# A mixture-of-experts layer whose 64 expert jobs are divided into 19 of 128 rows and 45 of 64 rows

## The chip, the cores and the metric

The kernel runs on one core of a Trainium2 chip. The metric is the device time of one launch in microseconds, from the first to the last work of the core. The matrix engine (TensorE) is PE in the profile, its weight loads are PEld, VectorE is DVE, ScalarE is ACT, GpSimd is POOL, and SyncE, which here only issues DMAs, is SP.

## What is computed

One layer of a decoder for 256 prompt tokens and 8 sample tokens, 264 in all, with a width of 1024. A token mixer of four branches comes first; behind it stands the mixture of experts that the change is about. All in fp32:

```python
scores = sigmoid(h @ router_w)
# 8 of 64 experts for each token, out of the 4 best of 8 groups of experts
gates  = 2.5 * scores of the chosen / their sum
hg  = einsum('nd,edf->nef', h, e_gate)      # e_gate, e_up: 64 x 1024 x 256
hu  = einsum('nd,edf->nef', h, e_up)
act = silu(hg) * hu * gates[:, :, None]
routed = einsum('nef,efd->nd', act, e_down) # e_down: 64 x 256 x 1024
x = x + gate2 * (routed + shared expert)    # then a final RMSNorm
```

With the inputs given, the routing sends between 0 and 118 tokens to an expert, 2112 in all. Nine of the 64 experts have over 64 tokens (118, 107, 106, 93, 84, 79, 76, 69, 68).

## The kernel before

The first 400 us are the token mixer, the routing and the shared expert; the change doesn't touch them. From then on the experts run as 64 jobs, one expert each, in 16 groups of `UNROLL` = 4. Groups 0, 1 and 2 are written out, 3 to 14 are a hardware loop, group 15 is written out again. Group 0 holds experts 0 to 3. All others are sorted by their token count on the chip, and `rank_of_job` tells which rank in this order a job takes.

**A job's shape.** A job has room for 128 rows (`CAP`) or for 64 (`HALF`). `is_large` decides: groups 0 and 1 whole, and from group 2 on the jobs j = 0 and j = 2. That makes 36 large and 28 small jobs. A job's products are

- `turn_rows`: 8 PE transposes of the rows that POOL gathered from HBM;
- `up`: the product with gate and up weights, 8 chunks k of 128. A large job in fp32 has 8 matmuls of 512 columns (L1039). A small one has 16 of 256 columns, in pairs that run side by side on the two halves of the array (L1041, L1042). The large jobs from group 2 on are *split* (`is_split`): for chunks 0 to 5 each factor is divided into a rounded high part and the rest, both fp32r, and three products of them are taken (`mm3`, L767), and only chunks 6 and 7 stay fp32 (L1039);
- `turn_act`: 2 transposes, and `down`: the product with the down weights, 4 matmuls of 512 columns for a large job (L1067), 4 in two pairs for a small one (L1072, L1075);
- `token_list`: 3 tiny matmuls (L985) that make the row list of a job in the group behind.

**The halves of the weights.** For a split job ACT writes the high parts of gate and up to `gu_high` in 3 pieces (`gu_highs`, L1390), and DVE then takes each off the weights in place (`gu_lows`, L1930). PE waits on `gu_lo` at every second chunk. There is one `gu_high`, so a job's pieces can be made once the split job ahead of it is through with its own.

**The order on PE** in slot j of group i: chunks 0 to 3 of up(i, j); turn_act of the job in front; chunks 4 to 7; turn_rows of the job behind; down of the job in front; token_list. ACT in the same slot: `act_out` of the job in front (L1365), `gate_out` (L1372), `rows_out` of the job behind (L1353 where split, L1358 else), `y_out` of the job in front (L1379). DVE: `one_hot`, `keep_scatter_row`, `gated` (L1884), `rows_out` (L1870, L1872 or L1875), `y_out` (L1892), `list_out` (L1850, L1851). Between these stand the pieces: for a split job two jobs behind, two high pieces at the end of the even slot and one in the odd slot, and the low ones in the odd slot. Each engine keeps the order as written.

**Loads.** SP reloads a weight slot (1 MB gate, 1 MB up, 1 MB down; four slots) when PE is done with it: gate and up wait on `up_done` of the job four back, down on `down_done`. POOL gathers a job's rows and scatter-adds its result, to `y_even` for even j and `y_odd` for odd j. `y_out` reuses the buffer of the job two back, and so waits until that one's scatter has landed (`scattered`).

Of the kernel before, what the change touches and what calls it, by code (L numbers as in the profile page):

```python
# [7 lines left out]
F32 = mybir.dt.float32  # L8
# [124 lines left out]
LARGE = 2 * UNROLL + (NE - 2 * UNROLL) // 2  # L133
# [9 lines left out]
def bass_decoder_step(nc, x_prompt, x_sample, state_conv, state_pool, state_conf, c_prompt, c_sample,  # L143
# [6 lines left out]
    with ExitStack() as ctx:  # L150
# [115 lines left out]
        cnt_f = sb("cnt_f", [P, 1])  # L266
# [17 lines left out]
        def in_mid(n):  # L284
# [56 lines left out]
                   silu_ready x_silu fin_red fin_sq dve_chain ld_mod sg_used  xgt_act xgt_dve actT_ready sort_in sort_rank sort_turned sort_back sort_out job_ready order_ready ld_prow xg_hi gu_hi gu_lo""".split()  # L341
# [78 lines left out]
        def is_large(i, j):  # L420

            return isinstance(i, int) and i < 2 or j % 2 == 0
# [4 lines left out]
        def is_split(i, j):  # L427
            return not (isinstance(i, int) and i < FIRST_SPLIT) and j % 2 == 0

        def pieces_until(i, j, p):  # L430

            return PIECES * (2 * (i - FIRST_SPLIT) + j // 2) + p + 1
# [13 lines left out]
        def extra_passes(eng, step):  # L446
            eng.wait_ge(S["cnt_ready"], 1)
            longest = eng.value_load(cnt_i[0:1, 0:1], min_val=0, max_val=TOK)
            with eng.If(longest > CAP):
                for r in range(1, ROUNDS):  # L450
                    with eng.Fori(0, NE) as e:
                        step(r, e, NE * (r - 1) + e)
# [5 lines left out]
        def _(sp):  # L458
# [117 lines left out]
            def extra(r, e, n):  # L576
                sp.wait_ge(S["x_xt"], n + 1)
                for at, view in ((0, gate_v), (2048, up_v), (4096, down_v)):
                    sp.dma_start(wexp[:, 0, at:at + 2048], view[bass.ds(e, 1)].rearrange("e p n -> (e p) n")).then_inc(S["x_w"], 16)
# [21 lines left out]
        def _(pool):  # L601
            n_chain = [0]

            def link(ins):
# [32 lines left out]
            g.iota(rank_of_job_i[:, 0:2 * UNROLL], pattern=[[1, 2 * UNROLL]], base=0, channel_multiplier=0)  # L637
            g.iota(rank_of_job_i[:, 2 * UNROLL:], pattern=[[2, NE // UNROLL - 2], [1, 2], [LARGE - 2 * UNROLL, 2]],
                   base=2 * UNROLL, channel_multiplier=0)
# [102 lines left out]
        def _(pe):  # L742
# [280 lines left out]
            def up(i, j, ks):  # L1023

                e = UNROLL * i + j
                x, w = xgT[j % 2], w_gu[j]
                if ks[0] == 0:
                    pe.wait_ge(S["xgt_act"], e + 1)
                    pe.wait_ge(S["xgt_dve"], e + 1)
                    pe.wait_ge(gu_full[j], 32 * (i + 1))  # L1030
                    need(pe, S["act_ready"], e - 1)
                for k in ks:
                    if is_split(i, j) and k < KS:
                        if k % 2 == 0:
                            pe.wait_ge(S["gu_lo"], pieces_until(i, j, k // 2))
# [88 lines left out]
            def extra(r, e, n):  # L1124
                pe.wait_ge(S["x_oh"], n + 1)
                for t in range(3):
                    rhs = tab[:, t, :, :].rearrange("p e c -> p (e c)")[:, bass.ds(2 * e, 2)]
                    last = mm(psum[:, LIST_BANK, 0:2], oh[:, 0, t, :], rhs, start=(t == 0), stop=(t == 2))
# [24 lines left out]
        def _(ac):  # L1153
# [191 lines left out]
            def rows_out(i, j):  # L1345
# [4 lines left out]
                if is_split(i, j):  # L1350
# [4 lines left out]
                    ac.wait_ge(S["xg_hi"], 2 * (2 * (i - FIRST_SPLIT) + j // 2) + 2)  # L1355
# [25 lines left out]
            def gu_highs(i, j, ps):  # L1381

                if not is_split(i, j):
                    return
                e = UNROLL * i + j
                if ps[0] == 0:
                    ac.wait_ge(gu_full[j], 32 * (i + 1))
                    ac.wait_ge(S["up_done"], e - 1)
                for p in ps:
                    F(as_r(gu_piece(gu_high, p)), gu_piece(w_gu[j], p), ACT.Copy).then_inc(S["gu_hi"], 1)  # L1390

            def body(i, first=False, last=False):
                for j in range(UNROLL):
                    prev = not (first and j == 0)
                    pi, pj = (i if j else i - 1), (j - 1) % UNROLL
                    ahead = (i if j < 2 else i + 1), 2 - j // 2 * 2
                    more = not (last and j >= 2)
# [9 lines left out]
                    if more and j % 2 == 0:  # L1407
                        gu_highs(*ahead, (0, 1))
# [30 lines left out]
        def _(ve):  # L1439
# [381 lines left out]
            V.tensor_reduce(cnt_f[:], b[:, 3 * NE:4 * NE], AX.X, ALU.max)  # L1821
# [3 lines left out]
            V.tensor_copy(cnt_i[:], cnt_f[:]).then_inc(S["cnt_ready"], 1)  # L1825
# [35 lines left out]
            def rows_out(i, j):  # L1861
# [4 lines left out]
                if is_split(i, j):  # L1866
                    for h in range(2):
                        k = min(4, KS - 4 * h)
                        ve.wait_ge(S["xg_hi"], 2 * (2 * (i - FIRST_SPLIT) + j // 2) + h + 1)
# [5 lines left out]
                V.tensor_copy(xgT[j % 2][:, 4:8, 0:n], psum[:, 6, :].rearrange("p (k c) -> p k c", k=4)[:, :, 0:n]).then_inc(S["xgt_dve"], 1)  # L1875

# [47 lines left out]
            def gu_lows(i, j, ps):  # L1924

                if not is_split(i, j):
                    return
                for p in ps:
                    ve.wait_ge(S["gu_hi"], pieces_until(i, j, p))
                    V.tensor_tensor(as_r(gu_piece(w_gu[j], p)), gu_piece(w_gu[j], p), as_r(gu_piece(gu_high, p)).bitcast(F32),  # L1930
                                    ALU.subtract).then_inc(S["gu_lo"], 1)

            def body(i, first=False, last=False):
                for j in range(UNROLL):
                    prev = not (first and j == 0)
                    pi, pj = (i if j else i - 1), (j - 1) % UNROLL
                    ahead = (i if j < 2 else i + 1), 2 - j // 2 * 2
                    more = not (last and j >= 2)
                    if more and j % 2:
                        gu_lows(*ahead, (0, 1))  # L1940
# [5 lines left out]
                    if more and j % 2:  # L1946
                        gu_lows(*ahead, (2,))
# [9 lines left out]
                    if not last:  # L1957
                        list_out(i + 1, j)

# [36 lines left out]

            def extra(r, e, n):
                for t in range(3):
                    last = V.tensor_scalar(oh[:, 0, t, :], row_order[0][:], posm[:, t, bass.ds(e, 1)], float(-CAP * r), ALU.subtract, ALU.is_equal)
                last.then_inc(S["x_oh"], 1)  # L2000
                ve.wait_ge(S["x_list"], n + 1)
                V.tensor_scalar(idx[:, 0, :], psum[:, LIST_BANK, 0:1], BIG, None, ALU.add)
                V.tensor_copy(gcol[:, 0, :], psum[:, LIST_BANK, 1:2]).then_inc(S["x_idx"], 1)
# [13 lines left out]
            extra_passes(ve, extra)  # L2017
# [42 lines left out]
```

## Time and profile before

| | us |
|---|---|
| median of 3 runs | 1051.63 (1049.86 to 1051.92) |
| the profiled execution, its time | 1049.66 |
| its span, first to last instruction | 1047.5 |
| PE busy | 975.9 (93%) |
| DVE busy | 593.7 (57%) |
| ACT busy | 375.4 (36%) |
| POOL busy | 233.3 (22%) |
| bytes by DMA | 305.60 MB |

The page gives busy time of each engine, then the span in 40 slices of 26.2 us, a digit for each. The chain of waits is the work that ended last, followed back: 91% of the span lies on PE. A timeline lists instructions with start and length; `xN` are N instructions in a row. Windows give busy time, granted TensorE clock (1.00 is 2.4 GHz, 0.50 is 1.2 GHz), the busy share of the 16 DMA engines and the bytes moved, for a stretch. The share is a sum of packet times, and packets of one engine can overlap, so it can pass 1.

### The profile page before, as it was taken

Reading aid. Unit: us, or ns where it says so; the run is one execution under the profiler, and the core shown is the slowest. Engines: PE = TensorE matmul, PEld = TensorE weight load, DVE = VectorE, ACT = ScalarE, POOL = GpSimd, SP = SyncE. Lnnn points to the kernel's source line nnn. Section 1 sums busy time; section 2 is a strip of 40 time slices with the busy share of each in tenths; the row PEclk is TensorE's granted clock in tenths of the full one; section 3 lists DMA queues with packets and bytes.
Section 4 is the critical chain, followed back from the end, with each engine's and each line's share of the span. In section 5 each row is a group of like instructions: output and inputs, shape, how many; then the busy total and the mean of one; then the engine's idle time right before and its main releaser. Section 6 shows DMA issues by size and latency. Waiting matters only on the chain.

```text
span 1047.5 us, 18756 instructions
## 1 busy us (share of the span) xinstructions
PE 975.9 (93%) x6321; PEld 696.1 (66%) x6321; DVE 593.7 (57%) x1346; ACT 375.4 (36%) x613; POOL 233.3 (22%) x172
## 2 busy tenths in 40 slices
PE   2799999999998898999999999999999999999980
PEld 1699999999997775444565655656565655656540
DVE  1656889999767444422445546464545545464517
ACT  3544444434462310112334333342424333242422
POOL 2000000000000001122333434343433434343322
PEclk9899999999999969999999999999999999999995
DMA  9975568687766275699999999999999999999813
GB/s 332 259 226 164 163 183 298 230 283 256 230 231 228 79 324 215 232 317 318 336 389 377 390 374 382 373 376 382 375 370 367 378 353 367 359 373 356 290 20 114
DMA packets 105674, 305.60 MB, mean 292 GB/s; under 512 B 15427, under 2 KB 57539, under 8 KB 80628
## 3 DMA queue, kind: packets, MB, share of 16 engines
q1 hardware_dynamic: 89715, 283.80, 73.2%
q0 software_dynamic: 15408, 19.69, 7.8%
q10 hardware_dynamic: 499, 1.40, 0.4%
q8 instruction: 35, 0.57, 0.2%
q14 instruction: 17, 0.14, 0.0%
HBM read 309.23 MB, written 31.42 MB: 325 GB/s over the span
## 4 chain that ended last, share of the span: by engine, by line
PE 91%; DVE 5%; DMA 2%; ACT 1%; issue 1%; ACTq 0%; SPq 0%; DVEq 0%; POOLq 0%
PE psum L767 36%; PE psum L1067 12%; PE psum L1039 10%; PE psum L1041 10%; PE psum L771 9%; PE psum L1072 5%; PE psum L786 2%; PE psum L957 2%; PE psum L985 1%; DMA bc<-in_norm_g 1%; PE psum L822 1%; PE psum L948 1%; PE psum L1005 1%; DVE wexp_r L1478 1%; DVE wexp L2015 1%
## 5 line engine op out<-in xcount | busy, mean ns | idle before, releaser
L767 PE MATMUL psum<-xn_r,wexp_r 128*128 128x264 f32 x1024 | 192.7, 288 | 2.2 <-DVE wexp_r L1478 2.2
L767 PEld LDWEIGHTS psum<-xn_r,wexp_r 128*128 128x128 f32 x1024 | 161.1, 191 | 4.8 <-DVE wexp_r L1478 2.7
L767 PE MATMUL psum<-hT_r,wexp_r 128*128 128x264 f32 x512 | 146.1, 285 | 0.0
L1884 DVE SCALAR_TENSOR_TENSOR hT<-psum,gcol,hT 128x256 f32<-128x256 f32 x64 | 30.6, 478 | 191.4 <-ACT hT L1372 191.4
L1067 PE MATMUL psum<-wexp,hT 128*128 128x512 f32 x288 | 129.7, 593 | 0.0
L1478 DVE TENSOR_TENSOR wexp_r<-wexp,wexp_r 128x1024 fp32r<-128x1024 f32 x88 | 106.6, 1219 | 27.2 <-ACT wexp_r L1206 26.9
L687 POOL DMA_INDIRECT y_odd<-mT,scatter_row x32 | 73.6, 2299 | 207.1 <-DVE gcol L1851 183.7
L767 PE MATMUL psum<-mod_room_r,mid_r 128*128 128x512 f32 x336 | 119.0, 409 | 0.0
L1039 PE MATMUL psum<-wexp,mid 128*128 128x512 f32 x240 | 110.8, 595 | 0.8 <-ACT mid L1358 0.8
L1206 ACT ACTIVATE wexp_r<-wexp 128x1024 fp32r<-128x1024 f32 x88 | 92.2, 1053 | 50.2 <-PE psum L767 42.5
L1041 PE MATMUL psum<-wexp,mid 128*64 128x256 f32 x448 | 108.6, 385 | 0.0
L1042 PE MATMUL psum<-wexp,mid 128*64 128x256 f32 x448 | 108.6, 385 | 0.0
L1930 DVE TENSOR_TENSOR wexp_r<-wexp,mod_room_r 128x1024 fp32r<-128x1024 f32 x84 | 99.8, 1216 | 15.1 <-ACT mod_room_r L1390 15.1
L1892 DVE COPY mT<-psum 128x512 f32<-128x512 f32 x64 | 44.0, 688 | 107.2 <-PE psum L1067 64.8
L767 PEld LDWEIGHTS psum<-hT_r,wexp_r 128*128 128x128 f32 x512 | 97.6, 191 | 0.1
L675 POOL DMA_INDIRECT xn<-h_table,idx x48 | 77.0, 1604 | 73.5 <-DVE gcol L1848 36.8
L1067 PEld LDWEIGHTS psum<-wexp,hT 128*128 128x128 f32 x288 | 52.0, 191 | 52.0 <-issue 52.0
L1390 ACT ACTIVATE mod_room_r<-wexp 128x1024 fp32r<-128x1024 f32 x84 | 85.2, 1046 | 0.0
L767 PE MATMUL psum<-wexp_r 128*128 128x264 f32 (+2 forms) x576 | 82.6, 284 | 2.7 <-DVE mT_r L1694 2.2
L687 POOL DMA_INDIRECT y_even<-mT,scatter_row x32 | 50.6, 1581 | 153.6 <-DVE gcol L1851 136.2
L1365 ACT ACTIVATE hT<-psum 128x256 f32<-128x256 f32 x64 | 21.6, 338 | 176.2 <-PE psum L771 174.9
L1041 PEld LDWEIGHTS psum<-wexp,mid 128*64 128x64 f32 x448 | 56.9, 136 | 29.3 <-issue 1.1
(291 smaller groups left out, 1490.7 us busy)
## 6 DMA issues: line engine op xcount, KB each, us to landing
wexp<-in_e_gate SPq DMA_DIRECT2D x64, 1024.0 KB, 8.1
wexp<-in_e_up SPq DMA_DIRECT2D x64, 1024.0 KB, 10.6
wexp<-in_e_down SPq DMA_DIRECT2D x64, 1024.0 KB, 9.6
wexp<-in_w_in SPq DMA_DIRECT2D x32, 1024.0 KB, 6.3
mid<-in_ada_w SPq DMA_DIRECT2D x8, 2048.0 KB, 9.5
wexp<-in_ada_w SPq DMA_DIRECT2D x4, 2048.0 KB, 20.1
wexp<-in_w_branch SPq DMA_DIRECT2D x8, 1024.0 KB, 5.0
wexp<-in_w_out SPq DMA_DIRECT2D x4, 1024.0 KB, 5.9
```

Of the source, the lines that this page charges most:

```text
L675: g.indirect_dma_start(out=xg[j][0:n], out_offset=None, in_=h_table, in_offset=bass.IndirectOffsetOnAxis(ap=idx[0:n, j, 0:1].bitcast(mybir ...
L687: g.indirect_dma_start(out=(y_even, y_odd)[j % 2], out_offset=bass.IndirectOffsetOnAxis(ap=scatter_row[0:n, j, :].bitcast(mybir.dt.uint32) ...
L767: last = mm(out, a[x], b[y], start=start and x == y == 0, stop=stop and x == 1)
L771: return nc.tensor.transpose(out, src, ident[0:rows, 0:rows])
L1039: last = mm(psum[:, j % 2, :].rearrange("p (a f) -> p a f", a=2), x[:, k, :], w[:, k], start=(k == 0), stop=(k == KT - 1))
L1041: mm(psum[HALF:CAP, j % 2, 0:FE], x[:, k, 0:HALF], w[:, k, 0], start=(k == 0), stop=(k == KT - 1), tile_position=(0, HALF))
L1042: last = mm(psum[0:HALF, j % 2, 0:FE], x[:, k, 0:HALF], w[:, k, 1], start=(k == 0), stop=(k == KT - 1), tile_position=(0, 0))
L1067: last = mm(psum[:, 3 + h, :], a[:, f, :], w[:, f, h * BLK:(h + 1) * BLK], start=(f == 0), stop=(f == 1))
L1206: F(as_r(high(u, q)), low(u, q), ACT.Copy).then_inc(S["w_hi"], 1)
L1390: F(as_r(gu_piece(gu_high, p)), gu_piece(w_gu[j], p), ACT.Copy).then_inc(S["gu_hi"], 1)
L1478: V.tensor_tensor(as_r(low(u, q)), low(u, q), as_r(high(u, q)).bitcast(F32), ALU.subtract).then_inc(S["w_lo"], 1)
L1930: V.tensor_tensor(as_r(gu_piece(w_gu[j], p)), gu_piece(w_gu[j], p), as_r(gu_piece(gu_high, p)).bitcast(F32), ALU.subtract).then_inc(S["gu_ ...
```

## The change

`is_large` and `is_split` now take j = 0 alone from group 1 on. Group 0 keeps four large jobs, every other group has one large and three small ones: 19 large, 45 small. The split jobs are j = 0 of groups 2 to 15, 14 in place of 28. `rank_of_job` gives the large jobs ranks 4 to 18 and the small ones the rest, three to a group. All three high pieces are now written behind the last operation of slot 3 of the group in front, and all three low pieces behind the last of slot 3 on DVE. `rows_beyond`, five small DVE instructions at the end of group 0, counts the experts with over 64 tokens, and `cnt_i` is set beyond 128 if there are more than 19 (experts 0 to 3 always count). In that case the passes behind the jobs, which also treat experts with over 128 tokens, run; they now go by jobs (`tab_job`, `posm_job`). With the inputs given the count is 12, so they don't run in either kernel.

```diff
-LARGE = 2 * UNROLL + (NE - 2 * UNROLL) // 2
+LARGE = UNROLL + (NE // UNROLL - 1)
...
         def is_large(i, j):
-            return isinstance(i, int) and i < 2 or j % 2 == 0
+            return isinstance(i, int) and i == 0 or j == 0
...
         def is_split(i, j):
-            return not (isinstance(i, int) and i < FIRST_SPLIT) and j % 2 == 0
+            return not (isinstance(i, int) and i < FIRST_SPLIT) and j == 0
...
-            def gu_highs(i, j, ps):
+            def gu_highs(i):
-                if not is_split(i, j):
+                if not is_split(i, 0):
                     return
-                e = UNROLL * i + j
-                if ps[0] == 0:
-                    ac.wait_ge(gu_full[j], 32 * (i + 1))
-                    ac.wait_ge(S["up_done"], e - 1)
-                for p in ps:
-                    F(as_r(gu_piece(gu_high, p)), gu_piece(w_gu[j], p), ACT.Copy).then_inc(S["gu_hi"], 1)
+                ac.wait_ge(gu_full[0], 32 * (i + 1))
+                need(ac, S["up_done"], UNROLL * (i - 1) + 1)
+                for p in range(PIECES):
+                    F(as_r(gu_piece(gu_high, p)), gu_piece(w_gu[0], p), ACT.Copy).then_inc(S["gu_hi"], 1)
...
                     if prev:
                         act_out(pi, pj)
-                    if more and j % 2:
-                        gu_highs(*ahead, (2,))
                     gate_out(i, j)
...
                     if prev:
                         y_out(pi, pj)
-                    if more and j % 2 == 0:
-                        gu_highs(*ahead, (0, 1))
+                    if j == UNROLL - 1 and not last:
+                        gu_highs(i + 1)
...
+            def rows_beyond():
+
+                link(V.tensor_scalar(keys[:, 1, :], keys[:, 0, :], float(NE * (HALF + 1)) - 0.5, None, ALU.is_gt))
+                link(V.tensor_reduce(cnt_f[:, 1:2], keys[:, 1, :], AX.X, ALU.add))
+                link(V.tensor_scalar(cnt_f[:, 1:2], cnt_f[:, 1:2], float(LARGE) + 0.5, float(TOK), ALU.is_gt, ALU.mult))
+                link(V.tensor_tensor(cnt_f[:, 0:1], cnt_f[:, 0:1], cnt_f[:, 1:2], ALU.max))
+                V.tensor_copy(cnt_i[:], cnt_f[:, 0:1]).then_inc(S["cnt_ready"], 1)
...
-                    if more and j % 2:
-                        gu_lows(*ahead, (0, 1))
...
-                    if more and j % 2:
-                        gu_lows(*ahead, (2,))
...
                     if not last:
                         list_out(i + 1, j)
+                    if first and j == UNROLL - 1:
+                        rows_beyond()
+                    if j == UNROLL - 1 and not last:
+                        gu_lows(i + 1)
```

Line numbers shift by up to 5 in the changed kernel. In the rows of order below, 128x2x64 or 64x256 marks a small job and 128x256 or 128x512 a large one. `hT` holds the activations of a job in this stage, `mT` its result, `mod_room_r` the high parts and `wexp_r` the low parts of the weights.

ACT, slots 2 and 3 of group 2, before:

```order
L1365 ACTIVATE hT<-psum 128x2x64
L1372 ACTIVATE hT<-psum 128x256
L1358 ACTIVATE mid<-psum 128x4x64
L1379 ACTIVATE mT<-psum 64x512
L1390 ACTIVATE mod_room_r<-wexp 128x1024 x2
L1365 ACTIVATE hT<-psum 128x256
L1390 ACTIVATE mod_room_r<-wexp 128x1024
L1372 ACTIVATE hT<-psum 64x256
L1353 ACTIVATE mid_r<-psum 128x512
L1353 ACTIVATE mid_r<-psum 128x256
L1379 ACTIVATE mT<-psum 128x512
```

and now:

```order
L1369 ACTIVATE hT<-psum 128x2x64
L1376 ACTIVATE hT<-psum 64x256
L1362 ACTIVATE mid<-psum 128x4x64
L1383 ACTIVATE mT<-psum 64x512
L1369 ACTIVATE hT<-psum 128x2x64
L1376 ACTIVATE hT<-psum 64x256
L1357 ACTIVATE mid_r<-psum 128x512
L1357 ACTIVATE mid_r<-psum 128x256
L1383 ACTIVATE mT<-psum 64x512
L1392 ACTIVATE mod_room_r<-wexp 128x1024 x3
```

The high pieces for job 0 of group 3 stood a slot ahead of the group's end, and now stand behind the last `y_out` of the group.

DVE, slot 3 of group 2 with the `y_out` and `list_out` in front of it, before:

```order
L1892 COPY mT<-psum 64x512
L1850 TENSOR_SCALAR idx<-psum 128x1
L1851 TENSOR_SCALAR gcol<-psum 128x1
L1930 TENSOR_TENSOR wexp_r<-wexp,mod_room_r 128x2x2x256 x2
L1835 TENSOR_SCALAR mid<-row_order_small,mid 128x64 x3
L1859 COPY scatter_row<-idx 64x1
L1930 TENSOR_TENSOR wexp_r<-wexp,mod_room_r 128x2x2x256
L1884 SCALAR_TENSOR_TENSOR hT<-psum,gcol,hT 64x256
L1870 TENSOR_TENSOR mid_r<-psum,mid_r 128x512
L1870 TENSOR_TENSOR mid_r<-psum,mid_r 128x256
L1872 COPY mid<-psum 128x256
L1892 COPY mT<-psum 128x512
```

and slot 3 now:

```order
L1832 TENSOR_SCALAR mid<-row_order_small,mid 128x64 x3
L1856 COPY scatter_row<-idx 64x1
L1889 SCALAR_TENSOR_TENSOR hT<-psum,gcol,hT 64x256
L1867 TENSOR_TENSOR mid_r<-psum,mid_r 128x512
L1867 TENSOR_TENSOR mid_r<-psum,mid_r 128x256
L1869 COPY mid<-psum 128x256
L1897 COPY mT<-psum 64x512
L1847 TENSOR_SCALAR idx<-psum 64x1
L1848 TENSOR_SCALAR gcol<-psum 64x1
L1935 TENSOR_TENSOR wexp_r<-wexp,mod_room_r 128x2x2x256 x3
```

The low pieces moved from the head of the slot to its end, behind `y_out` and `list_out`.

PE, from the last slot of group 1 to the first products of group 2, before:

```order
L1039 MATMUL psum<-wexp,mid 128x512 x4
L771 MATMUL psum<-ident,xn 128x128 x8
L1067 MATMUL psum<-wexp,hT 128x512 x4
L985 MATMUL psum<-mid 64x6 x3
L767 MATMUL psum<-mod_room_r,mid_r 128x512
L767 MATMUL psum<-wexp_r,mid_r 128x512
```

and now:

```order
L1045 MATMUL psum<-wexp,mid 64x256
L1046 MATMUL psum<-wexp,mid 64x256
L775 MATMUL psum<-ident,xn 128x128 x8
L1076 MATMUL psum<-wexp,hT 64x512
L1079 MATMUL psum<-wexp,hT 64x512
L1076 MATMUL psum<-wexp,hT 64x512
L1079 MATMUL psum<-wexp,hT 64x512
L989 MATMUL psum<-mid 64x6 x3
L771 MATMUL psum<-mod_room_r,mid_r 128x512
L771 MATMUL psum<-wexp_r,mid_r 128x512
```

In front of the split products now stands a small `down` and not a large one; the first product of the high parts is what waits on the pieces.

## Rows read from the trace of the kernel before

**Rows 1.** The page: busy time of PE; clock and DMA share in 40 slices.

```profile
PE 975.9 (93%) x6321; PEld 696.1 (66%) x6321; DVE 593.7 (57%) x1346; ACT 375.4 (36%) x613; POOL 233.3 (22%) x172
...
PEclk9899999999999969999999999999999999999995
DMA  9975568687766275699999999999999999999813
```

**Rows 2.** Chain of waits in one group (start, length, what), from a split job.

```profile
707.99 2.95 PE psum L767 x12
...
715.15 0.57 PE psum L1072
...
717.18 0.36 PE psum L1041
...
722.47 3.44 PE psum L1067 x8
725.90 0.19 PE psum L985 x3
726.09 2.99 PE psum L767 x12
...
735.33 0.36 PE psum L1041
...
744.23 2.95 PE psum L767 x12
```

**Rows 3.** The same chain in group 1 and at the start of group 2.

```profile
472.12 3.54 PE psum L1039 x8
...
507.20 2.95 PE psum L767 x12
...
517.85 0.36 PE psum L1041
```

**Rows 4.** Timeline of ACT behind a small down (start, length, what, idle before).

```profile
717.04 0.59 ACT L1379 ACTIVATE mT<-psum 64x512 f32<-64x512 f32 x1 [1.48 <-PE psum L1075]
717.54 1.99 ACT L1390 ACTIVATE mod_room_r<-wexp 128x1024 fp32r<-128x1024 f32 x2
```

**Rows 5.** Timeline of DVE at the same place.

```profile
717.83 0.27 DVE L1851 TENSOR_SCALAR gcol<-psum 128x1 f32<-128x1 f32 x1
718.62 2.36 DVE L1930 TENSOR_TENSOR wexp_r<-wexp,mod_room_r 128x1024 fp32r<-128x1024 f32 x2 [0.52 <-ACT mod_room_r L1390]
```

**Rows 6.** Windows: stretch, length, busy of each engine, PEclk, DMA share, GB/s.

```profile
372.00:388.00 16.00, 16.00 (x67) 11.78 (x65) 8.85 (x57) 3.29 (x7) 0.00 (x0) 0.72 1.01 424
544.80:581.00 36.20, 36.20 (x194) 21.77 (x192) 18.49 (x46) 13.43 (x24) 14.28 (x8) 1.00 1.02 385
943.00:979.00 36.00, 36.00 (x192) 21.80 (x192) 18.58 (x46) 13.43 (x24) 14.26 (x8) 1.00 0.96 352
467.90:993.40 525.50, 525.50 (x2703) 312.62 (x2702) 260.78 (x643) 190.46 (x340) 197.88 (x113) 1.00 0.98 365
```

**Rows 7.** SP: an issue of weights; its waits from 600 to 950 us; landing (page).

```profile
467.93 0.34 SPq L535 DMA_DIRECT2D wexp<-in_e_gate  x1
...
SPq L535 <- PE psum L1039: 101.4, 20, 5.2
...
wexp<-in_e_up SPq DMA_DIRECT2D x64, 1024.0 KB, 10.6
```

**Rows 8.** POOL's scatters from 500 to 990 us, from issue to landing.

```profile
DMA to landing us min/median/max: 6.4/8.3/10.2
```

**Rows 9.** Windows around idle time of PE: busy of PE comes first.

```profile
320.00:324.00 4.00, 1.80 (x16) 1.16 (x15) 3.96 (x7) 2.14 (x3) 0.00 (x0) 1.00 0.88 288
386.00:391.20 5.20, 3.33 (x28) 3.16 (x27) 2.38 (x14) 0.00 (x0) 0.00 (x0) 1.00 0.60 246
391.20:394.60 3.40, 3.40 (x9) 2.58 (x8) 0.97 (x5) 0.00 (x0) 1.11 (x1) 0.50 0.11 25
```

More of the change, by code:

```diff
@@ L265, in bass_decoder_step @@
         zeros = sb("zeros", [P, P])
-        cnt_f = sb("cnt_f", [P, 1])
+        cnt_f = sb("cnt_f", [P, 2])
         cnt_i = sb("cnt_i", [P, 1], I32)
@@ L441, in bass_decoder_step, with extra_passes @@
         fin_y = wexp[:, 1, :].rearrange("p (a t d) -> p a t d", a=2, t=3)
-        def extra_passes(eng, step):
+        def extra_passes(eng, step, prepare=None):
             eng.wait_ge(S["cnt_ready"], 1)
@@ L449, in extra_passes @@
             with eng.If(longest > CAP):
+                if prepare:
+                    prepare()
                 for r in range(1, ROUNDS):
@@ L574, in _, with extra @@
             load_down(final, UNROLL - 1)
-            def extra(r, e, n):
+            def extra(r, job, n):
                 sp.wait_ge(S["x_xt"], n + 1)
+                e = sp.value_load(order_i[0:1, bass.ds(job, 1)], min_val=0, max_val=NE - 1)
                 for at, view in ((0, gate_v), (2048, up_v), (4096, down_v)):
@@ L1126, in extra @@
                 for t in range(3):
-                    rhs = tab[:, t, :, :].rearrange("p e c -> p (e c)")[:, bass.ds(2 * e, 2)]
-                    last = mm(psum[:, LIST_BANK, 0:2], oh[:, 0, t, :], rhs, start=(t == 0), stop=(t == 2))
+                    rhs = tab_job[:, t, :, :].rearrange("p e c -> p (e c)")[:, bass.ds(LISTC * e, LISTC)]
+                    last = mm(psum[:, LIST_BANK, 0:LISTC], oh_job[:, 0, t, :], rhs, start=(t == 0), stop=(t == 2))
                 last.then_inc(S["x_list"], 1)
@@ L1395, in body @@
                     pi, pj = (i if j else i - 1), (j - 1) % UNROLL
-                    ahead = (i if j < 2 else i + 1), 2 - j // 2 * 2
-                    more = not (last and j >= 2)
                     if prev:
                         act_out(pi, pj)
-                    if more and j % 2:
-                        gu_highs(*ahead, (2,))
                     gate_out(i, j)
@@ L1922, in sort_out, with gu_lows @@
                 ve.wait_ge(S["job_ready"], 1)
-            def gu_lows(i, j, ps):
-                if not is_split(i, j):
+            def gu_lows(i):
+                if not is_split(i, 0):
                     return
-                for p in ps:
-                    ve.wait_ge(S["gu_hi"], pieces_until(i, j, p))
-                    V.tensor_tensor(as_r(gu_piece(w_gu[j], p)), gu_piece(w_gu[j], p), as_r(gu_piece(gu_high, p)).bitcast(F32),
+                for p in range(PIECES):
+                    ve.wait_ge(S["gu_hi"], pieces_until(i, p))
+                    V.tensor_tensor(as_r(gu_piece(w_gu[0], p)), gu_piece(w_gu[0], p), as_r(gu_piece(gu_high, p)).bitcast(F32),
                                     ALU.subtract).then_inc(S["gu_lo"], 1)
@@ L1936, in body @@
                     pi, pj = (i if j else i - 1), (j - 1) % UNROLL
-                    ahead = (i if j < 2 else i + 1), 2 - j // 2 * 2
-                    more = not (last and j >= 2)
-                    if more and j % 2:
-                        gu_lows(*ahead, (0, 1))
                     if not prev:
@@ L2016, in _ @@
                 V.tensor_tensor(x_sb[0:n, t, :], x_sb[0:n, t, :], fin_y[0:n, 0, t], ALU.add).then_inc(S["even_taken"], 1)
-            extra_passes(ve, extra)
+            extra_passes(ve, extra, shift_small)
             for t in range(2):
```

33 lines of the change are left out of this document (19 added, 14 removed).

## The prediction

> **What bounds the kernel now.** I read the page first, then the chain of waits, then windows of the stage that the change touches. The page has PE busy for 93% of the span, and its clock at 9 tenths or more in every slice of the expert stage [rows 1]. The chain inside that stage is PE from end to end: piece follows piece with no step on another engine [rows 2, 3], and the window from 467.9 to 993.4 us has PE busy for all of its 525.50 us at clock 1.00 [rows 6]. So PE is the bound, and each microsecond taken off it counts until something else is late. What is late next shows in the same windows: the DMA engines have a share of 0.96 to 1.02 while they move 352 to 385 GB/s [rows 6]. Yet SP spends its time waiting for PE to free a slot [rows 7]. DMA is close behind PE, not ahead of it. ACT and DVE have room on average; the question there is one of place, not of load.
>
> **Part 1: the shapes of jobs on PE.** Slots are read off the chain [rows 2]. From the first split product to the first small product is the split slot: 717.18 - 707.99 = 9.19 us; it holds the small down of the job in front. From there to the next split job is a small slot with a large down: 726.09 - 717.18 = 8.91. A group is 744.23 - 707.99 = 36.24 us. The new kernel needs a slot that this trace doesn't have: a small job behind a small job. It is the small slot without its large down and list (726.09 - 722.47 = 3.62) and with the small down and list (717.18 - 715.15 = 2.03) in their place: 8.91 - 3.62 + 2.03 = 7.32. A new group of PE work is 9.19 + 8.91 + 2 x 7.32 = 32.74, so 3.50 less. For the 14 groups from 2 to 15 that is 49.0 us. All parts of the 7.32 are measured, only their meeting is not; 0.2 either way on 28 such slots is 5.6 us, and I keep that for the range.
>
> Group 1 goes from four fp32 large jobs to one. Jobs 5 to 7 took 507.20 - 472.12 = 35.08 us [rows 3]; now they take 8.91 + 2 x 7.32 = 23.55, so 11.53 less. The first slot of group 2 had a large down in it (517.85 - 507.20 = 10.65) and is now a plain split slot, 1.46 less. PE work removed: 49.0 + 11.5 + 1.5 = 62.0 us.
>
> **Part 2: the halves are made too late.** This is what the added order costs. The three high pieces now stand behind `y_out` of slot 3, which waits for the small down that is PE's last work but the list before the split job. Nothing else is left for PE to do meanwhile. The trace already has this very row of events, in the even slots, where the pieces were for a job a slot further on and cost nothing. There the small down began at 715.15 and the list was over at 717.18, which is when PE would now ask for piece 0 [rows 2]. ACT started `y_out` at 717.04 and the high pieces at 717.54 [rows 4]. DVE was through with the list at 718.10 and began the low pieces at 718.62, 2.36 us for two, so 1.2 each: piece 0 is ready at about 719.84 [rows 5]. PE stands still for 719.84 - 717.18 = 2.66 us. The next pieces come every 1.2 us while PE takes 2.95 / 2 = 1.47 us for a piece [rows 2], so they cost nothing more. Bounds: 2.4 if the pieces follow `y_out` without the half microsecond of handing over, 3.4 if each handing over takes twice as long as here. I take 2.66, since the row is of the same instructions in the same order. Fourteen times: 37.2 us.
>
> Behind the waiting PE is queued the whole split slot, and through it the release of weight slots to SP. Behind the high pieces on ACT is `act_out` of the last job, which PE asks for only four chunks later; behind the low pieces on DVE is a one-hot that is asked for at the slot's end. Both are covered by the split products. ACT also waits for gate and up to have landed, but these were issued a group ahead (below).
>
> **Part 3: waits that come nearer.** `y_out` of job 2 waits for the scatter of job 0. The distance shrinks from 18.1 to 2 x 7.32 = 14.6 us. The scatter is issued under 1 us behind `y_out` and lands in at most 10.2 [rows 8], so 3 us are left and I put no cost. `rows_beyond` has five small DVE instructions in an fp32 slot of 11.6 us in which DVE is mostly idle: nothing. The extra passes stay off, with 12 against 19.
>
> **Part 4: DMA.** A group's bytes are 36.2 us x 385 GB/s = 13.9 MB early and 36.0 x 352 = 12.7 MB late, of which 12.6 are weights [rows 6]. The new group takes 32.74 + 2.66 = 35.4 us, so it asks for 394 GB/s early and 358 late. The only stretch with a true backlog (eight loads issued at once, no row traffic) ran at 424 [rows 6], and the best with row traffic at 385. If 385 were a ceiling, an early group would need 36.2 us, 0.8 more than PE. The reserve covers that: a load issued at 467.93 [rows 7] was first used at 507.20; with group 1 shorter by 11.5 it is used at 495.7, which is 27.7 us later, and it lands in 10.6 [rows 7]. So 17 us of reserve against 14 x 0.8 = 11. No cost in the sum, and the term with the least margin. The Trainium skill (Perfetto Trace Analysis, Roofline) gives a single core about 435 GB/s over its 16 DMA engines; that is near the 424 of this trace, and by it the early group would be an estimated 32 us of DMA, so it speaks for no cost too.
>
> **The sum.** 1049.66 (the profiled execution's time) - 62.0 + 37.2 = 1024.9 us. That execution lies 1.97 below the median, so against the median the forecast is 1051.63 - 24.8 = **1026.8 us**. With slots and stall at their bounds it is 1020 to 1036.
>
> **Rivals.**
>
> *DMA becomes the bound.* For it: a share of 0.98 over 525 us, with 365 GB/s [rows 6]. Against it: 424 GB/s under backlog, and the reserve. If today's mean pace is already all that this mix of loads, gathers and scatters gives, the stretch doesn't shrink and only the reserve of 17.1 us is gained: 1034.5.
>
> *The pieces are not late* (the engines find the time after all). Nothing in the order allows it, as `y_out` stands ahead on both engines. Then PE would save all 62, but 13.9 MB in 32.7 us are 426 GB/s, and DMA binds: 191.8 MB (365 x 525.5) at 385 take 498 us, 27 less, plus the reserve of 17: 1007.
>
> *The clock falls in the new idle time*; this ends on the other side. Each group now has one gap of 2.66 us on PE, where there was none. The trace is divided: with 2.2 us idle of 4.0 the clock stayed at 1.00, but behind a stretch with 1.9 us idle of 5.2, much of the rest transposes, it stood at 0.50 for 3.4 us [rows 9]. A low stretch of length L costs L/2, and 14 of them eat the gain of 24.8 from L = 3.5 on. With 3.4 each the time is 1026.8 + 23.8 = 1050.6, no change; with 6.8 each, 1074. Against it speaks that the gap here is set between dense products. The Trainium skill (TensorE: Matmul & The Clock Gate, HAM oscillation) tells of kernels that wait in each turn of a loop and start each turn at the low clock. [...]
>
> *The change doesn't do what it says*: more than 19 experts over 64 rows would start 128 more passes. The routing of these inputs excludes it.
>
> **How the numbers follow.** Forecast (1020 to 1036) 0.66; DMA bound 0.16; pieces not late 0.05; clock low for about 3.4 us a group 0.05; clock low for longer 0.06; something else that loses more than is gained 0.02. A measurement of this kernel can tell about 0.2% from no change, 2 us. Faster: 0.66 + 0.16 + 0.05 = 0.87. Same: 0.05. Slower: 0.08. The range takes the forecast's bounds, widened by 2 us below for a stall at its lower bound, and up to 1042 for a DMA bound that meets slots at their upper bound: 1018 to 1042.
>
> **What would show it.** Right: one idle gap on PE in front of each split job and none elsewhere, released by the low pieces on DVE, 14 of about 2.7 us; small slots of 7.3 us; a group period of 35.4; DMA share at 1.00 or more. Wrong: gaps in front of small jobs, released by loads or by `xn` gathers (DMA); slots of 7.3 stretched evenly at a clock below 1.00 (clock); `y_out` waiting for a scatter (part 3); a stall that differs between early and late groups. What would make the forecast wrong most easily is the length of the stall, since 0.5 us on it is 7 us.

## The result, and the profile after

The changed kernel takes **1044.99 us** (median of 6 runs, 1043.22 to 1047.25); the kernel before took 1051.16 beside it (6 runs, 1049.72 to 1051.92). The ratio is 0.9948, with an interval of 0.9932 to 0.9963. So it is faster by only 0.5%, clear of the noise: 6.2 us where 24.8 were forecast, and outside the range that ended at 1042. The profiled execution took 1045.04 us, with a span of 1043.3.

The page of the changed kernel answers to [rows 1]. Its rows are: PE's busy time; the clock and the DMA share in 40 slices; the chain by engine; PE's busiest group with what ended the idle time ahead of it.

```profile
PE 926.4 (89%) x6509; PEld 675.8 (65%) x6509; DVE 531.7 (51%) x1280; ACT 326.2 (31%) x557; POOL 192.3 (18%) x173
...
PEclk9899999999999969999999998999999999999995
DMA  9975558787667185689999999999999999999712
...
PE 81%; DMA 8%; DVE 7%; ACT 3%; issue 1%; ACTq 0%; SPq 0%; DVEq 0%; POOLq 0%
...
L771 PE MATMUL psum<-mod_room_r,mid_r 128*128 128x512 f32 x168 | 71.3, 485 | 45.4 <-DVE wexp_r L1935 45.4
```

PE is busy for 926.4 us, and the chain now has parts that aren't PE: DVE and ACT (the pieces) and DMA. In the waits of PE from 490 to 985 us there is one row alone (what waited, for what; total, times, longest):

```profile
PE psum L771 <- DVE wexp_r L1935: 45.4, 14, 6.2
```

Fourteen waits, one in front of each split job, as forecast. Twelve of them last 2.81 to 2.99 us. The chain at the first of them (start, length, what), to be laid beside [rows 2, 4, 5]:

```profile
495.95 0.06 PE psum L1079
...
496.49 1.05 ACT mod_room_r L1392
497.54 0.02 issue
497.56 1.24 DVE wexp_r L1935
498.80 0.14 issue
498.93 3.02 PE psum L771 x12
```

PE stands still for 2.9 us: 0.5 until ACT begins, 1.05 for the high piece, 1.24 for the low piece, 0.14 to hand over. The next two such places, the first from the chain and the last too, show what comes on top. The first is an ordinary gap behind which the 12 products take 4.58 us in place of 3.02. The second is a gap of 6.25 us:

```profile
569.78 1.24 DVE wexp_r L1935
571.02 0.04 issue
571.07 4.58 PE psum L771 x12
...
614.57 0.33 SPq L537
...
615.01 29.31 DMA wexp<-in_e_up
644.32 0.02 issue
644.34 1.06 ACT mod_room_r L1392
645.41 0.02 issue
645.43 1.24 DVE wexp_r L1935
646.67 0.04 issue
646.71 1.65 PE psum L771 x3
```

Here the up weights landed 29.31 us behind their issue (median 10.6 before [rows 7]), and ACT waited for them. Windows of the changed kernel, columns as in [rows 6]:

```profile
500.00:940.00 440.00, 402.75 (x2421) 248.45 (x2419) 167.19 (x488) 117.08 (x238) 131.58 (x96) 0.96 0.98 372
534.70:538.10 3.40, 3.40 (x9) 2.63 (x8) 2.33 (x6) 0.04 (x1) 2.21 (x2) 0.50 1.02 366
572.20:575.60 3.40, 3.40 (x10) 2.52 (x9) 1.73 (x5) 0.00 (x0) 1.61 (x2) 0.50 1.01 384
646.70:650.10 3.40, 3.39 (x8) 2.72 (x9) 2.88 (x6) 0.59 (x1) 0.00 (x0) 0.50 1.02 360
650.70:656.30 5.60, 5.60 (x28) 3.82 (x28) 0.76 (x2) 1.04 (x3) 0.00 (x0) 1.00 0.57 219
```

Behind 10 of the 14 gaps PE's clock is at 0.50, the 1.2 GHz level, for 3.4 us (once for 6.8, of which 2.8 lie in the long gap itself). The stage of before held 1.00 throughout [rows 6].

From the first split job (498.93) to the last (977.75) are 13 groups in 478.82 us, 36.83 each; the forecast had 35.40, so 460.2. The missing 18.6 us are about the whole error of the forecast (18.2). The rows split it so: idle gaps of 2.90 for 2.66 (3.1), two gaps lengthened by loads (6.25 and 4.43: 4.9), and, as the remainder, slow clock with less PE work per group (32.44 instead of 32.74, which gives 3.9 back): 14.5. Whether these are causes, and what is late next, was put to the chip.

### The profile page after: what moved, and what is told of

It reads as the page before. It is cut to its first block, busy times and chain, and to the rows that moved or that the text cites. A ratio compares the mean times of both kernels' runs of the same rounds, so it can differ in the third digit from the quotient of the medians.

```text
span 1043.3 us, 18868 instructions
## 1 busy us (share of the span) xinstructions
PE 926.4 (89%) x6509; PEld 675.8 (65%) x6509; DVE 531.7 (51%) x1280; ACT 326.2 (31%) x557; POOL 192.3 (18%) x173
## 3 DMA queue, kind: packets, MB, share of 16 engines
q0 software_dynamic: 13232, 19.68, 7.9%
## 4 chain that ended last, share of the span: by engine, by line
PE 81%; DMA 8%; DVE 7%; ACT 3%; issue 1%; ACTq 0%; SPq 0%; DVEq 0%; POOLq 0%
PE psum L771 32%; PE psum L1045 11%; PE psum L775 9%; PE psum L1076 7%; PE psum L1043 6%; PE psum L1071 6%; DMA wexp<-in_e_up 5%; PE psum L1046 3%; PE psum L790 2%; PE psum L961 2%; DVE wexp_r L1935 2%; ACT mod_room_r L1392 1%; DMA bc<-in_norm_g 1%; PE psum L826 1%; PE psum L952 1%
## 5 line engine op out<-in xcount | busy, mean ns | idle before, releaser
L1046 PE MATMUL psum<-wexp,mid 128*64 128x256 f32 x720 | 174.0, 384 | 0.0
L1045 PE MATMUL psum<-wexp,mid 128*64 128x256 f32 x720 | 173.8, 384 | 0.0
L1889 DVE SCALAR_TENSOR_TENSOR hT<-psum,gcol,hT 128x256 f32<-128x256 f32 (+1 forms) x64 | 30.6, 478 | 240.0 <-ACT hT L1376 176.4
L1045 PEld LDWEIGHTS psum<-wexp,mid 128*64 128x64 f32 x720 | 92.4, 136 | 38.5 <-issue 5.9
L771 PE MATMUL psum<-mod_room_r,mid_r 128*128 128x512 f32 x168 | 71.3, 485 | 45.4 <-DVE wexp_r L1935 45.4
L1897 DVE COPY mT<-psum 128x512 f32<-128x512 f32 (+1 forms) x64 | 43.7, 683 | 103.7 <-PE psum L1071 57.5
L1046 PEld LDWEIGHTS psum<-wexp,mid 128*64 128x64 f32 x720 | 91.5, 137 | 0.0
L1076 PE MATMUL psum<-wexp,hT 128*64 128x512 f32 x180 | 86.8, 604 | 0.5 <-ACT hT L1369 0.5
L1079 PE MATMUL psum<-wexp,hT 128*64 128x512 f32 x180 | 86.8, 604 | 0.0
L691 POOL DMA_INDIRECT y_odd<-mT,scatter_row x32 | 46.3, 1447 | 218.0 <-DVE gcol L1848 115.8
L1369 ACT ACTIVATE hT<-psum 128x256 f32<-128x256 f32 (+1 forms) x64 | 19.7, 308 | 196.2 <-PE psum L775 194.3
L771 PEld LDWEIGHTS psum<-wexp_r 128*128 128x128 f32 (+1 forms) x576 | 72.2, 177 | 6.1 <-DVE mT_r L1692 2.5
L771 PEld LDWEIGHTS psum<-mod_room_r,mid_r 128*128 128x128 f32 x168 | 38.9, 232 | 55.3 <-DVE wexp_r L1935 40.6
L775 PEld LDWEIGHTS psum<-ident,xn 128*128 128x128 f32 (+1 forms) x432 | 54.6, 193 | 29.5 <-issue 22.5
```

What stands on the lines that cost most here:

```text
L691: g.indirect_dma_start(out=(y_even, y_odd)[j % 2], out_offset=bass.IndirectOffsetOnAxis(ap=scatter_row[0:n, j, :].bitcast(mybir.dt.uint32) ...
L771: last = mm(out, a[x], b[y], start=start and x == y == 0, stop=stop and x == 1)
L775: return nc.tensor.transpose(out, src, ident[0:rows, 0:rows])
L1076: left = mm(psum[HALF:CAP, 3, :], a[:, f, 0:HALF], w[:, f, 0:BLK], start=(f == 0), stop=(f == 1), tile_position=(0, HALF))
L1079: right = mm(psum[0:HALF, 4, :], a[:, f, 0:HALF], w[:, f, BLK:], start=(f == 0), stop=(f == 1), tile_position=(0, 0))
L1897: V.tensor_copy(y_rows[0:n, j % 2, BLK:2 * BLK], psum[0:n, 4, :]).then_inc(S["ys_dve"], 1)
```

## Experiments

All times are medians beside the kernel before (1050.9 to 1051.3 in these comparisons); ratios are against it.

### The pieces earlier

The order of ACT and DVE is changed; nothing else. The expectations below call this kernel e1_early.

```
 ACT, slot 2, at its end:            + gu_highs(i + 1, (0, 1))
 ACT, slot 3, behind act_out:        + gu_highs(i + 1, (2,))
 ACT, slot 3, behind y_out:          - gu_highs(i + 1)
 DVE, slot 3, at its start:          + gu_lows(i + 1, (0, 1))
 DVE, behind keep_scatter_row:       + gu_lows(i + 1, (2,))
 DVE, slot 3, at its end:            - gu_lows(i + 1)
```

> The changed kernel with the pieces made earlier: high pieces 0 and 1 at the end of slot 2, piece 2 in slot 3, low pieces in slot 3, as the kernel before had them for its job 0. Job shapes as changed. In the changed kernel's trace PE has 14 gaps of 2.9 us ahead of the split jobs, the clock falls behind most of them (9 stretches of 3.4 us, about 1.6 us lost each), and two gaps are longer by 3.4 and 1.5 us, ended by a load. Theory A (the late pieces cost gap and clock, but the DMA is close behind): gaps gone, clock at 1.00 through the expert stage, and the DMA becomes the bound at 385 GB/s or so; time 1003 to 1020 us. Theory B (PE alone bounds it): 14 x 2.9 + 15 + 5 us less, about 985 us. Theory C (the DMA already bounds the changed kernel, the gaps only hide it): within 0.5% of the changed kernel's 1045 us.

Measured: 1036.08 us (1035.65 to 1037.38), ratio 0.9867 (0.9850 to 0.9884). Only 8.9 us were gained, and the time fits none of the three theories. PE no longer waits for a low piece itself. Its waits from 500 to 940 us, its window, and a link of its chain:

```profile
PE psum L771 <- DVE mid L1872: 21.2, 12, 2.7
PE psum L1076 <- ACT hT L1369: 15.9, 5, 8.1
```

```profile
500.00:940.00 440.00, 402.93 (x2424) 246.18 (x2423) 168.26 (x492) 120.84 (x240) 124.52 (x97) 0.96 0.99 374
...
535.96 29.26 DMA wexp<-in_e_up
```

The idle time has moved, to what stands behind the pieces. On DVE the last chunks of the split job's own rows (L1872) come behind all three low pieces, twelve times up to 2.7 us late. ACT, in order, now waits for the up weights with the high pieces at its head, and the activated rows of a small job (L1369) come up to 8.1 us late behind it. PE is busy for 403 of 440 us at clock 0.96, as it was in the changed kernel. The late pieces had hidden a second bound, the loads.

### PE kept busy in the gap

```
 PE, behind the list of slot 3, when the next job is split:
+    need(pe, S["act_ready"], UNROLL * (i + 1) - 1)
+    for _ in range(3):
+        mm(psum[:, 0, :], ident[:, :], bc[:, 3, 0:BLK], start=True, stop=True)   # thrown away
```

> The changed kernel with three extra fp32 products of 512 columns on PE ahead of each split job (2.6 us of work on data that is thrown away, into the PSUM bank that the split job then overwrites), where PE stands idle for 2.9 us now. Nothing is made earlier. If the fall of the clock is a cost of its own, caused by the idle gap: clock 1.00 through the stage, a group period of 35.3 us in place of 36.9, and 12 to 17 us less than the changed kernel, about 1030 us, unless the DMA takes a part of it back. If the clock has nothing to do with it: the same time as the changed kernel, 1045, or a little more.

Measured: 1035.83 us (1034.67 to 1036.81), ratio 0.9859 (0.9841 to 0.9877). The window answers to the first one above:

```profile
500.00:940.00 440.00, 429.22 (x2516) 256.31 (x2515) 173.85 (x499) 121.79 (x243) 136.13 (x98) 1.00 0.99 377
```

Products that compute nothing make the kernel 9.2 us faster. The clock is at 1.00 but for one stretch of 3.4 us at 686.8, behind a gap of 3.5 us that a load made; a gap of 3.40 us at 644.3 has no fall behind it. So it was the idle time that let the clock fall. PE still waits now and then; the chain leads the two longest of these waits (3.40 and 3.51 us) back to up weights that landed 31.4 and 29.4 us behind their issue:

```profile
PE psum L771 <- DVE wexp_r L1939: 7.8, 4, 3.5
PE psum L1045 <- DMA wexp<-in_e_up: 2.0, 1, 2.0
```

### No split jobs, and the pieces ahead of the output copies

The first has `is_split` return False: the large jobs use fp32 products and there are no pieces. The second keeps the pieces in slot 3 but ahead of `y_out`:

```
 ACT:  - if prev: y_out(pi, pj)
       - if j == UNROLL - 1 and not last: gu_highs(i + 1)
       + if j == UNROLL - 1 and not last: gu_highs(i + 1)
       + if prev: y_out(pi, pj)
 DVE:  gu_lows(i + 1) in the same way ahead of y_out
```

> The changed kernel without any split job: the 14 split jobs are plain fp32 large jobs, there are no pieces to wait for and no work of halves on ACT and DVE. Up of such a job takes 6.98 us where the split one takes 6.06, so PE work per group is about 33.4 us. Theory A (gap and clock, DMA close behind): no gaps, clock 1.00, DMA bound, 1003 to 1020 us, about the same as e1_early. Theory B (PE alone): about 998 us. Theory C: 1045.

> The changed kernel with the pieces still in slot 3 but ahead of y_out on ACT and DVE. The high pieces no longer wait for the small down; piece 0 should be ready about 1.2 us behind the list, so the gap is 1.2 us in place of 2.9. If the clock falls only behind the longer gap, it stays at 1.00 here. Then the group period is 33.6 us on PE and the DMA bounds: 1003 to 1025 us. If any gap makes it fall, the period is 35.3 and the time about 1022.

Measured: 1033.30 us without split jobs (1031.44 to 1035.54; ratio 0.9838, 0.9814 to 0.9861), and 1033.09 with the pieces ahead (1031.30 to 1033.99; ratio 0.9829, 0.9810 to 0.9848). Neither time was expected: both lie at least 8 us above the ranges with the DMA as bound, and 12 below theory C. PE's waits in the stage, without split jobs and then with the pieces ahead:

```profile
PE psum L1043 <- DMA wexp<-in_e_up: 21.8, 10, 4.6
PE psum L1045 <- DMA wexp<-in_e_up: 1.6, 3, 1.0
```

```profile
PE psum L771 <- DVE wexp_r L1935: 37.3, 14, 5.5
PE psum L1045 <- DMA wexp<-in_e_up: 2.8, 1, 2.8
```

Four kernels with quite different PE work end between 1033 and 1036 us, and without pieces PE waits for loads alone. From 500 to 940 us they move 374 to 378 GB/s, where before and after move 372. These are the two best versions found that compute the whole result, 1.6 to 1.7% faster than before; between them there is no difference.

The clock is part of this floor. It stays at 1.00 in the filled kernel alone; its mean is 0.96 with early pieces, 0.97 without split jobs and 0.98 with the pieces ahead, since the waits for loads are idle time too. With the pieces ahead, the nine gaps in front of split jobs that last 1.5 to 1.9 us have no fall behind them, and the five of 3.2 us and more have one each. Without split jobs it fell behind a wait of 1.90 us as well (timeline and window):

```profile
863.19 5.39 PE L1043 MATMUL psum<-wexp,mid 128*128 128x512 f32 x8 [1.90 <-DMA wexp<-in_e_up]
...
863.50:866.80 3.30, 3.30 (x5) 1.28 (x4) 0.00 (x0) 0.00 (x0) 1.89 (x2) 0.50 1.00 412
```

### Half of the down weights left out

```
-  sp.dma_start(wexp[:, s, 4096:6144], rows_of_expert(down_v, e))
+  n = 1024 if light_now[0] else 2048        # light from group 1 on
+  sp.dma_start(wexp[:, s, 4096:4096 + n], rows_of_expert(down_v, e)[:, 0:n])
```

This takes 31.4 MB of 283.8 off the loads' queue and leaves every instruction of PE in place. It is put on four kernels: early pieces, the new kernel, the new kernel with filled gaps, and the kernel before.

> e1_early with half of the down weights of each expert left out of the loads from group 1 on (0.5 MB of 3 MB a job; the other half of the slot keeps old data, so a part of the computation is done on other weights). PE's work is unchanged. If the DMA is what bounds e1_early at 1036 us, its bytes fall by 16% and PE becomes the bound: group period 32.5 us, no waits for loads, clock 1.00, about 985 to 992 us. If something else keeps e1_early up (POOL, the order on DVE or ACT), it stays near 1036.

> The new kernel as it is (late pieces, nothing thrown away on PE), with half of each down weight left out of the loads from group 1 on; it computes on other weights. DMA can't bind here. Theory (the late pieces cost the 2.90 us of idle time and the slow clock behind it, whatever DMA does): against the early pieces under light loads (996.1) a group takes 2.2 us more idle time and about 1.2 us of slow clock, so 996 + 14 x 2.2 + 10 x 1.65 = 1043; without the 4.9 us in which the new kernel waited for loads, 1040 at best. Rival 1 (the clock falls only because DMA stretches the idle time): clock 1.00, group period 35.4, 1027. Rival 2 (the gap is mostly DMA's doing): the gaps shrink under 1.5 us, 1010 or less.

> The same light loads, and three products thrown away on PE ahead of each split job, so that PE is not idle while it waits for the pieces. Theory: this is the forecast's own arithmetic with neither clock nor DMA in it: group period 32.44 + 2.90 = 35.34 at clock 1.00, so 996 + 14 x 2.2 = 1027 (1023 to 1031). Against the filled kernel with full loads (1035.8) the difference of about 9 us is DMA. Rival (the filled kernel already ran at PE's pace, and its other 9 us over the forecast lie in PE's work): no difference, 1034 to 1036.

> The kernel before with the same light loads. Theory (before is bound by PE in the whole stage, group period 36.24 read off the chain): 1049 to 1052, no change. Rival (DMA already stretched the kernel before, so that its chain was no measure of PE's work): 1040 or less.

| kernel | full loads | light loads | ratio to before, light |
|---|---|---|---|
| early pieces | 1036.08 | 996.12 (994.88 to 997.48) | 0.9475 (0.9459 to 0.9490) |
| new kernel | 1044.99 | 1040.18 (1038.17 to 1041.39) | 0.9891 (0.9873 to 0.9908) |
| new, gaps filled | 1035.83 | 1025.51 (1024.16 to 1026.56) | 0.9759 (0.9742 to 0.9775) |
| before | 1050.88 | 1051.39 (1049.34 to 1052.12) | 1.0003 (0.9994 to 1.0013) |

The windows from 500 to 940 us, of early pieces, the new kernel and the filled one, all with light loads:

```profile
500.00:940.00 440.00, 428.81 (x2654) 264.06 (x2654) 183.22 (x532) 131.12 (x263) 154.10 (x106) 1.00 0.96 346
```

```profile
500.00:940.00 440.00, 404.26 (x2434) 249.64 (x2435) 173.41 (x496) 121.31 (x242) 138.93 (x98) 0.97 0.90 320
```

```profile
500.00:940.00 440.00, 438.60 (x2583) 261.27 (x2583) 174.86 (x508) 123.14 (x248) 139.99 (x99) 1.00 0.92 327
```

The table takes the result apart. With neither slow clock in the stage nor waits for loads the new kernel takes 1025.51 us; the forecast was 1026.8. The clock adds 1040.18 - 1025.51 = **14.7 us**, over nine slow stretches of 3.4 us in that trace, so 1.63 each. The full loads add 1044.99 - 1040.18 = **4.8**, which includes what slow clock their longer waits bring. The waits of the new kernel with light loads show 14 gaps, none over 3.0 us:

```profile
PE psum L775 <- DVE wexp_r L1939: 40.6, 14, 3.0
```

Three of the four expectations held; the early pieces ended at 996.12, a little above the 985 to 992 expected, and their trace has 11 us of waits for the split job's rows (L1876, 10.8 us in 12 times). The first row of the table is the other half of the story: with early pieces the full loads cost 40 us, waits and the slow clock behind them together (clock 0.96 with them, 1.00 without). And the last row says that before was bound by PE alone.

### Scatters left out, and the order of rows

The pieces stand ahead of `y_out`, and the 64 scatters leave out all rows but those of token 0:

```
-    bounds_check=last_token, oob_is_err=False, compute_op=ALU.add)
+    bounds_check=first_token, oob_is_err=False, compute_op=ALU.add)    # first_token = 0
```

> The pieces ahead of the output copies, full loads, and the scatters of the 64 jobs leave out all rows but those of token 0 (their bound is 0): weights and gathers as they are. Theory (weights, gathers and scatters together fill the DMA engines, and the scatters' rows are the part that is spread badly): the time falls from 1033.1 towards PE's own pace of about 1010 with 1.6 us gaps; 1010 to 1020. Rival 1 (the ceiling is set by the weight bytes alone): 1030 to 1034. Rival 2 (it is the gathers that collide with the loads): above 1025 with 8-engine stretches still there.

Measured: 1007.97 us (1007.68 to 1008.81), ratio 0.9591 (0.9575 to 0.9607), 25.1 less than with the scatters. PE's waits in the stage, and the window:

```profile
PE psum L773 <- DVE wexp_r L1937: 23.2, 14, 1.8
PE psum L1078 <- ACT hT L1371: 0.5, 1, 0.5
```

```profile
500.00:940.00 440.00, 419.92 (x2620) 257.58 (x2618) 181.34 (x531) 128.66 (x258) 128.18 (x104) 1.00 0.99 384
```

No wait for loads is left, only the gap of the pieces, now 1.66 us, and the clock doesn't fall behind it. What was left out are 8.6 MB (the row queue goes from 19.68 to 11.07), 23 us of DMA time at the 378 GB/s of the kernel with scatters. The time ended just under the 1010 to 1020 of the theory, and both rivals are out. The scatters are worth about their bytes; but the clock went back from 0.98 to 1.00 as well, so the 25.1 us don't split cleanly. The theory said more, that their rows are badly spread over the DMA engines; the time alone doesn't need it.

That part was tried by changing which row of a large job stands at which place (e6_early_spread and the two that follow it):

```
-  g.iota(order_large_i.rearrange("p (a b m l) -> p a b m l", a=2, b=2, m=8), pattern=[[8, 2], [64, 2], [1, 8], [16, 4]], ...)
+  g.iota(order_large_i, pattern=[[1, 16], [16, 8]], ...)
```

> e1_early with another order of the rows of a large job: the token positions go to rows 0, 8, 16, ... in place of rows 0, 4, ..., 28 and 64, 68, ..., 92, so that few tokens lie on rows of all parts of the tile and not of one half of them. In all kernels with waits for loads there are stretches with exactly 8 of 16 DMA engines at work (2 to 6 us long, some 25 us in sum). If the row order loads one half of the engines more with row traffic, these stretches go and the time falls by 5 to 15 us, to 1021 to 1031. If it doesn't, 1036 within 0.3%.

> The changed kernel with the row order of e6_early_spread and nothing else. Its two longer gaps (6.2 and 4.4 us) are ended by loads; with balanced engines they would be 2.9 like the others: 5 us less, about 1040. The gaps of 2.9 us and the clock falls behind them stay.

> The kernel before with the row order of e6_early_spread and nothing else. PE never waits there, so whatever it does for the DMA engines it can't shorten the time: 1051 within 0.2%.

Measured: early pieces 1055.30 us (1053.90 to 1058.42; ratio 1.0047, 1.0030 to 1.0064), new kernel 1056.42 (1056.37 to 1059.38; 1.0062, 1.0041 to 1.0082), before 1066.03 (1064.15 to 1068.96; 1.0138, 1.0119 to 1.0157). That is 19.2, 11.4 and about 15 us **more**, where less or nothing was expected. The window of before as it was, and with this order:

```profile
500.00:940.00 440.00, 440.00 (x2320) 264.77 (x2319) 224.23 (x553) 162.32 (x291) 169.79 (x97) 1.00 0.99 372
500.00:940.00 440.00, 426.20 (x2229) 255.47 (x2228) 211.95 (x533) 158.27 (x280) 130.89 (x94) 1.00 0.96 357
```

The same bytes move at 357 GB/s, and PE, never idle there before, now waits; from 640 to 740 us the chain leads three of these waits back to up weights that landed 24 to 26 us behind their issue. So the places of the rows do matter to DMA, and the order in use is better than the even spread tried here. The expectation had it the wrong way round.

The packets in the traces say more. From 500 to 940 us exactly eight packets are in flight for 1.0 us in the kernel before, 13.0 in the new one, 12.8 with early pieces and 12.6 with the pieces ahead (not the 25 of the expectation). The changed order makes this 18.5 in the kernel before, 28.6 in the new one and 25.8 with early pieces; without the scatters' rows it is 2.8 instead of 12.6. So these stretches, like the window at 650.70 above with a share of 0.57 and a pace of 219 GB/s, hang on the row traffic and its order. That rows of few tokens fall on half of the 16 engines, and the other half stands idle, would fit all of it; but packets of one engine can overlap, and no run shows which engine carries which row, so this stays open.

## Why the prediction was wrong

**PE bounds the kernel before.** Right: taking 31 MB off its loads changes nothing (ratio 1.0003).

**Part 1, shapes.** Right within 0.3 us a group: 36.93 - 2.90 - 1.6 = 32.43 for a group with one slow stretch, 35.34 - 2.90 = 32.44 for one without, and 32.74 were forecast. A slot of a small job behind a small job takes 7.13 us instead of 7.32.

**Part 2, late pieces.** Right in place, number and cause. 2.90 us instead of 2.66: DVE began the low piece 1.53 us behind PE's last product (1.44 in the row it was taken from), and the step from DVE to PE took 0.14, which the sum didn't have. Together 3.4 us over 14 gaps, about what part 1 gave back (14 x 0.3 = 4.2). That 1025.5 comes so near to 1026.8 is thus in part two small errors that cancel. The stated bounds, 0.2 on 28 slots and a stall of 2.4 to 3.4, add up to 1017.6 to 1042.8 and not to the 1020 to 1036 of the sum; 1045 lies outside of both.

**The clock: the step that failed.** The prediction weighed this rival with a price that was nearly right (3.4 us a stretch, half of it lost) and gave that price 0.05 and a longer fall 0.06, because "the gap here is set between dense products". That sentence was no evidence: [rows 9] had one idle stretch with a fall and one without, far too few for it. The stretch without one was moreover the luck of one execution. It lies in the part that the change doesn't touch, with the same wait of 2.19 us in every kernel, and in 6 of the 14 traces the clock falls behind it. The stretch right behind it in the kernel before, and in the same kernel with light loads, where 3.4 of the 4.6 us are at 0.50:

```profile
324.00:328.60 4.60, 4.42 (x39) 3.25 (x37) 4.60 (x5) 3.36 (x4) 0.00 (x0) 1.00 1.03 373
324.00:328.60 4.60, 4.45 (x27) 2.69 (x25) 4.60 (x5) 3.46 (x4) 0.00 (x0) 0.63 1.00 382
```

The other runs show that the products around don't protect: 14.7 us lost with 2.9 us gaps, none when the gaps were filled, none with 1.66 us gaps. It was not every gap: with light loads 9 of 14 had a fall behind them, and of the twelve that last 2.90 us seven. What decides between equal gaps no run here was made to show. The sum needed a term of 9 x 1.63 = 14.7 us; it had nothing. The Trainium skill (TensorE: Matmul & The Clock Gate, HAM oscillation) tells of loops that wait in each turn and start each turn slow. The prediction set this against its own rows and sided with the rows. That page words its rule for idle gaps longer than the 2.66 us forecast here; the trace agrees with its direction for two gaps of three, at a shorter gap than it names, and with 3.4 us rather than the 6.8 of the rival's worse end.

**Part 4, DMA: the second step that failed.** Forecast were 17 us of reserve and no cost. The reserve was sized well: at the first wait a landing had grown from the 10.6 of [rows 7] to 29.3 us, by 18.7. But it was spent by group 6. The pace of the mix was taken as 385, from the best window of before with row traffic; 372 to 378 is what every kernel with full loads and the rows' own order holds over 440 us. The mean of before, 365 [rows 6], was only what its PE asked for, yet it was nearer to the ceiling than the best window, so that part of the rival "DMA becomes the bound" was the better guess. It cost 4.8 us here because PE had been slowed by its own gaps; with early pieces it cost 40. That rival gave 1034.5, and 1033 to 1036 is where the kernel lands when the gaps are mended. The agreement is luck in part: its sum had neither the slow clock that three of these kernels have nor the thrown-away products of the fourth. The Trainium skill (Perfetto Trace Analysis, Roofline) gives about 435 GB/s for one core; over 440 us with row traffic no run passed 384, and the measurement decides.

**Where the expected gain went.** PE's work fell by the 62 us forecast and some 4 more; 40.6 were handed back as idle time, where 37.2 were forecast; 14.7 went to the clock; 4.8 to the loads. Moving the pieces alone can't bring the rest: the four mended kernels gain 9 to 12 us of the 49 which PE offers (1045 to 996). In three of them waits for loads, with slow clock behind them, stand in the way. In the filled one only 10.3 us are the loads' (1035.83 to 1025.51), and the rest is the thrown-away work.

## What to carry to other kernels

A repeated idle gap on TensorE is to be priced with the clock behind it, half of each slow stretch; one gap without a fall is no evidence, since equal gaps differ, from turn to turn and from one execution to the next, and thrown-away products in the gap are a quick test. When the bound engine loses work, don't take the second engine's pace from its best window; making its load lighter, in one run, shows what it costs. Before moving pieces of work forward on an engine that runs in order, see what they wait for: what stands behind them inherits that wait.

## What the runs showed of the hardware

- The clock fell to 1.2 GHz behind gaps of 2.9 us and longer, for 3.4 us each (6.8 once in the new kernel), and not behind gaps of 1.66 us. Of twelve gaps of 2.90 us (new kernel, light loads) seven had a fall behind them and five had none. The shortest wait in the expert stage with a fall behind it was 1.90 us (no split jobs).
- The same wait of 2.19 us, ahead of the expert stage, had a fall behind it in 6 of 14 traces.
- Loads of 1 MB each, with row gathers and scatters beside them, move at 372 to 378 GB/s over 440 us, at a share of 0.98 to 0.99, whether PE waits for them or not; with most of the scatters' rows left out, 384. Under this load a transfer that had landed in 10.6 us took 29.
- The order in which a job's rows lie moves the whole kernel by 11 to 19 us, with the same bytes, and the time with exactly eight packets in flight by 13 to 18 us.
